# Two-layer hybrid encoder: sums of block products moved to GpSimd, half of the keys copied by transfers

## The reference

```python
h = rmsnorm(x, norm_g)
proj = jnp.einsum('bsd,de->bse', h, w_in)
aq, ak, av, ag, bq, bk, bv, bg = jnp.split(proj, SPLITS, axis=-1)
ya = chunk_relbias_attention(aq, ak, av, rel_bias) * silu(ag)   # 16 heads of 64, own chunk of 64 + previous 8
yb = swa_sink_gqa(rope(bq), rope(bk), bv, sinks) * silu(bg)     # 16 query heads, 2 key heads, window 128
x = x + concat(ya, yb) @ w_out
```

## Time and profile before

| what | value |
| --- | --- |
| median of 3 runs | 1610.96 us (1610.89 to 1611.48) |
| the profiled execution | 1612.55 us, its span 1610.2 us |
| mean granted clock of TensorE | 0.993 |
| busy: TensorE, VectorE, ScalarE, GpSimd | 99%, 79%, 59%, 30% of the span |
| HBM traffic | 109 GB/s over the span |

### The profile page before, as it was taken

The page is one execution under the profiler, slowest core; times in us unless marked ns, Lnnn a source line. Parts: engine busy times, 40 slices in busy tenths (PEclk is TensorE's granted clock), DMA queues, the critical chain, the costliest instruction groups (busy, mean ns, idle before and its releaser), DMA issues.

```text
span 1610.2 us, 29380 instructions
## 1 busy us (share of the span) xinstructions
PE 1589.0 (99%) x9541; PEld 1418.0 (88%) x9541; DVE 1276.6 (79%) x2631; ACT 954.7 (59%) x1977; POOL 477.5 (30%) x666
## 2 busy tenths in 40 slices
PE   9899999999999999999999999999999999999997
PEld 7799999999888888899988999999988888888997
DVE  7987788887677777888878788788876787888875
ACT  7766666667556666433466666766665566663333
POOL 0754454453222100010046445445422212000000
PEclk9999999999999999999999999999999999999998
DMA  6233323323523322344432332323343233223343
GB/s 223 79 97 104 109 85 109 104 90 114 167 92 95 113 88 92 105 152 157 164 104 73 107 107 91 110 90 104 109 157 112 92 107 103 79 99 112 131 144 118
DMA packets 77511, 180.69 MB, mean 112 GB/s; under 512 B 9408, under 2 KB 13792, under 8 KB 70640
## 3 DMA queue, kind: packets, MB, share of 16 engines
q1 hardware_dynamic: 76960, 178.99, 33.3%
q10 hardware_dynamic: 432, 0.55, 0.1%
q0 software_dynamic: 32, 0.08, 0.0%
HBM read 163.25 MB, written 11.62 MB: 109 GB/s over the span
## 4 chain that ended last, share of the span: by engine, by line
PE 91%; DVE 6%; DMA 1%; issue 1%; ACT 1%; SPq 0%; DVEq 0%; ACTq 0%
PE ps_proj L730 10%; PE ps_proj L732 10%; PE ps_proj L731 10%; PE ps_proj L892 4%; PE ps_proj L893 4%; PE ps_proj L894 4%; PE ps_proj L905 3%; PE ps_proj L906 2%; PE ps_proj L907 2%; PE ps_o L800 2%; PE ps_t L787 2%; PE ps_s L892 2%; PE ps_s L894 2%; PE ps_s L893 2%; PE ps_t L894 2%; PE ps_t L893 2%
## 5 line engine op out<-in xcount | busy, mean ns | idle before, releaser
L1110 ACT ACTIVATE w_hi<-w_raw 128x512 fp32r<-128x512 f32 (+1 forms) x528 | 385.7, 743 | 198.5 <-DVE w_raw L1986 62.5
L1581 DVE TENSOR_TENSOR w_lo<-w_raw,w_hi 128x512 fp32r<-128x512 f32 (+1 forms) x528 | 459.4, 878 | 34.0 <-ACT w_hi L1110 29.9
L730 PE MATMUL ps_proj<-act_hi,w_hi 128*128 128x512 f32 x704 | 276.9, 393 | 0.0
L731 PE MATMUL ps_proj<-act_lo,w_hi 128*128 128x512 f32 x704 | 274.8, 390 | 0.0
L732 PE MATMUL ps_proj<-act_hi,w_lo 128*128 128x512 f32 x704 | 274.7, 390 | 0.0
L2315 POOL TENSOR_TENSOR w_raw<-w_raw 128x128 f32<-128x128 f32 x140 | 92.0, 657 | 300.1 <-DMA w_raw<-w 299.9
L732 PEld LDWEIGHTS ps_proj<-act_hi,w_lo 128*128 128x128 f32 x704 | 132.1, 188 | 28.4
L1110 ACT ACTIVATE arena<-ps_t 128x512 fp32r<-128x512 f32 (+4 forms) x168 | 75.3, 453 | 135.3 <-PE ps_t L787 82.9
L730 PEld LDWEIGHTS ps_proj<-act_hi,w_hi 128*128 128x128 f32 x704 | 132.5, 188 | 24.8
L731 PEld LDWEIGHTS ps_proj<-act_lo,w_hi 128*128 128x128 f32 x704 | 132.4, 188 | 24.3
L1175 ACT ACTIVATE probs<-probs,nmax 128x128 f32<-128x128 f32 (+3 forms) x128 | 72.1, 563 | 97.3 <-DVE nmax L1653 95.4
(11 more groups left out here) (398 smaller groups left out, 4688.4 us busy)
## 6 DMA issues: line engine op xcount, KB each, us to landing
w_raw<-w SPq DMA_DIRECT2D x322, 256.0 KB, 3.0
w_raw<-w SPq DMA_DIRECT2D x51, 1024.0 KB, 4.9
temp<-temp SPq DMA_DIRECT2D x72, 64.0 KB, 4.0
strips_tables<-ext SPq DMA_DIRECT2D x16, 256.0 KB, 3.9
temp<-xT SPq DMA_DIRECT2D x16, 256.0 KB, 4.4
xs<-xy SPq DMA_DIRECT2D x16, 256.0 KB, 4.3
temp<-xs SPq DMA_DIRECT2D x16, 256.0 KB, 4.1
strips_tables<-ext SPq DMA_DIRECT2D x16, 224.0 KB, 4.4
```

Of the source, the lines that this page charges most:

```text
L730: pe.matmul(dst, wh, act_hi[:, k, :], start=start, stop=False)
L731: pe.matmul(dst, wh, act_lo[:, k, :], start=False, stop=False)
L1110: return nc.scalar.activation(dst, src, ACT.Copy, scale=scale)
L1581: return nc.vector.tensor_tensor(dst, src, hi, ALU.subtract)
```

## The change

- ScalarE now copies the whole bank of P1 and P6 to `in_w1`, VectorE the whole bank of P5 and P7, halves exchanged, to `in_w2` (`move_products`), and GpSimd makes the four additions there (`sum_products`), behind piece 10's weight sums for the first pair and behind piece 2's of the next unit for the second. TensorE waits for the two copies in place of the sums.
- `hi_k` and `lo_k` fill one half of the partitions each; two transfers of 256 KB per unit, issued by SP (`copy_k`), fill the other. SP issues them behind the load of piece 20. TensorE waits for their landing.
- At the start of a layer the row sums' lows 2, 3 and 4 move behind the take of the last tile and into pieces 0 and 1 of unit 1, and the reciprocal of the root moves ahead of that piece's weight subtraction.

```diff
-H_SUMS_AT = (10, 11, 12, 14, 15)
+H_SUMS_AT = (10, 11, 13, 14)
+H_SUMS_AFTER = {1: 1, 3: 2, 4: 4}
+KEYS_BEHIND = 20
...
+            def copy_k(v):
+
+                sp.wait_ge(k_done, v + 1)
+                carry_wait(sp)
+                for h in range(2):
+                    own, other = slice(64 * h, 64 * h + 64), slice(64 - 64 * h, P - 64 * h)
+                    sp.dma_start(k_st[other, :, h, :].bitcast(F32), k_st[own, :, h, :].bitcast(F32)).then_inc(k_copied, 16)
...
                 load_strips(L, 0)
+                copy_k(L * V_LAYER)
                 for j in range(4, Y_BEHIND):
                     load_in(T, L, 1, j)
...
                         if j == STRIPS_BEHIND:
                             load_strips(L, u)
+                        if j == KEYS_BEHIND:
+                            copy_k(L * V_LAYER + u)
...
                 load_strips(L, PAIRS - 1)
+                copy_k(L * V_LAYER + (PAIRS - 1))
...
                 for s in range(4):
+                    if s == 3:
+                        copy_k(L * V_LAYER + PAIRS)
                     prefetch(T + A_SLOTS, s)
...
                 if e == 0:
                     pe.wait_ge(q_done, g + 1)
-                    pe.wait_ge(k_done, v + 1)
+                    pe.wait_ge(k_copied, (v + 1) * 32)
...
                     if i == 0:
-                        pe.wait_ge(in_summed, q * 4 + 4)
+                        pe.wait_ge(in_copied, q + 1)
+                        pe.wait_ge(in_moved, q + 1)
...
                 for h in range(2):
-                    for half in range(2):
+                    for half in (h,):
                         last = copy(k_hi2[64 * half:64 * half + 64, h, :], t_k[64 * h:64 * h + 64, :])
...
                 else:
                     act.wait_ge(h_summed, (L * (IN_SUM_K - 1) + m) * 4)
-                    act.wait_ge(h_sum_lo, (L * IN_SUM_K + m) * 2)
+                if m in H_SUMS_AFTER:
+                    act.wait_ge(h_sum_lo, (L * IN_SUM_K + H_SUMS_AFTER[m]) * 2)
...
-                copy(in_w1[:, 0:SEQ // 2], in_banks(p // 8)[1][0][:, 0:SEQ // 2]).then_inc(in_copied, 1)
+                copy(in_w1, in_banks(p // 8)[1][0][:, :]).then_inc(in_copied, 1)
...
+                    if p == 1 and first:
+                        hi_h_sums(L, IN_SUM_K - 1)
...
-                    for half in range(2):
+                    for half in (h,):
                         last = low(k_lo2[64 * half:64 * half + 64, h, :], t_k[own, :], k_hi2[own, h, :].bitcast(F32))
...
-            def sum_of_products_in(L, u, p):
...
+            def move_products(L, u, p):
+
+                in_passed(dve, L, u, p // 8 * 8 + 5)
+                bank_of = in_banks(p // 8)[1][1][:, :].rearrange("p (h c) -> p h c", h=2)
+                dst = in_w2.rearrange("p (h c) -> p h c", h=2)
+                nc.vector.tensor_copy(dst[:, ::-1, :], bank_of).then_inc(in_moved, 1)
...
-                dve.wait_ge(in_summed, q * 4 + 8)
+                dve.wait_ge(in_summed, q * 4 + 4)
...
-                    if p == 0 and first:
-                        lo_h_sums(L, IN_SUM_K - 1)
+                    if p < 2 and first:
+                        lo_h_sums(L, p + 3)
...
+                        if p == 2 * PTS + 2:
+                            invert_root(L)
                         if p == 3 * PTS:
                             take_rstd(L)
                         duties(T, L, p, ("a_first", pair_a(L, 0), L * V_LAYER))
...
-                        if p == 2 * PTS + 2:
-                            invert_root(L)
-                        if p in H_SUMS_AT[:-1]:
+                        if p in H_SUMS_AT[:2]:
                             lo_h_sums(L, H_SUMS_AT.index(p))
                 dve.wait_ge(k_done, L * V_LAYER + 1)
                 take(T, 3, t_v, ps=ps_t[1])
                 dve.wait_ge(proj_free, T + 4)
                 dve.sem_inc(rows_added, 2)
+                lo_h_sums(L, 2)
...
+            def sum_products(L, u, half):
+
+                q = pair_in(L, u, half * 8)
+                (w1l, w1r), (w2l, w2r) = left_right(in_w1), left_right(in_w2)
+                pool.wait_ge(in_copied, q + 2)
+                carry_wait(pool)
+                pool.wait_ge(in_moved, q + 2)
+                carry_wait(pool)
+                nc.gpsimd.tensor_tensor(w1r, w1l, w1r, ALU.add).then_inc(in_summed, 1)
+                pool.wait_ge(in_summed, q * 4 + 1)
+                nc.gpsimd.tensor_tensor(w2l, w2l, w1r, ALU.add).then_inc(in_summed, 1)
+                pool.wait_ge(in_summed, q * 4 + 2)
+                nc.gpsimd.tensor_tensor(w1r, w2r, w1r, ALU.add).then_inc(in_summed, 1)
+                pool.wait_ge(in_summed, q * 4 + 3)
+                nc.gpsimd.tensor_tensor(w2r, w2r, w2l, ALU.add).then_inc(in_summed, 1)
+
+            def sums_of_unit(L, u, first=False):
+                for j in range(16):
+                    if IN_CHUNKS[j % 8][0] == "s":
+                        sum_w_in(L, u, j)
+                    if j == 2 and not first:
+                        sum_products(L, u - 1, 1)
+                    if j == 10:
+                        sum_products(L, u, 0)
```

More of the change, by code:

```diff
@@ L233, in trunk @@
         in_copied = sem("in_copied")
+        in_moved = sem("in_moved")
         in_summed = sem("in_summed")
@@ L269, in trunk @@
         k_done = sem("k_done")
+        k_copied = sem("k_copied")
         swapped = sem("swapped")
@@ L809, in scores_b @@
                 if n == 0:
-                    pe.wait_ge(k_done, L * V_LAYER + V_LAYER)
+                    pe.wait_ge(k_copied, (L * V_LAYER + V_LAYER) * 32)
                 pe.wait_ge(biased, step_b(L, n))
@@ L1069, in _ @@
                     unit_sums(T + u * 4, L, u, att_a(L, u - 1))
-                pe.wait_ge(in_summed, (L + 1) * (IN_PAIRS * 4) + 4)
+                pe.wait_ge(in_copied, (L + 1) * IN_PAIRS + 1)
+                pe.wait_ge(in_moved, (L + 1) * IN_PAIRS + 1)
                 unit(T + A_SLOTS, att_a(L, PAIRS - 1))
@@ L1338, in copy_p1, with unit_sums @@
                 act.wait_ge(rows_added, q * 2 + (2 * L + 2))
-                copy(in_w1[:, 0:SEQ // 2], in_banks(p // 8)[1][0][:, 0:SEQ // 2]).then_inc(in_copied, 1)
-            def unit_sums(T, L, u, att, g):
+                copy(in_w1, in_banks(p // 8)[1][0][:, :]).then_inc(in_copied, 1)
+            def unit_sums(T, L, u, att, g, first=False, last=False):
                 for p in range(16):
                     def other():
-                        if isinstance(u, int) and p + HI_AHEAD >= 16:
+                        if last and p + HI_AHEAD >= 16:
                             hi_next(tile0(L) + A_SLOTS, L, p + HI_AHEAD - 16)
@@ L1423, in squares_first @@
                     nc.scalar.activation(sq_first(j), xy[:, j, :], ACT.Square).then_inc(sq_done, 1)
+            act.sem_inc(in_copied, 1)
             act.dma_start(gain_sb[:, :], gains).then_inc(gains_in, 16)
@@ L1488, in _ @@
                         duties(T, L, p, ("a_first", pair_a(L, 0)))
-                with act.Fori(1, PAIRS - 1) as u:
+                unit_sums(T + 4, L, 1, att_a(L, 0), pair_a(L, 1), first=True)
+                with act.Fori(2, PAIRS - 1) as u:
                     unit_sums(T + u * 4, L, u, att_a(L, u - 1), pair_a(L, u))
-                unit_sums(T + (PAIRS - 1) * 4, L, PAIRS - 1, att_a(L, PAIRS - 2), pair_a(L, PAIRS - 1))
+                unit_sums(T + (PAIRS - 1) * 4, L, PAIRS - 1, att_a(L, PAIRS - 2), pair_a(L, PAIRS - 1), last=True)
                 unit(T + A_SLOTS, L, att_a(L, PAIRS - 1), ("b", None))
@@ L1808, in lo_next @@
                 low(w_lo[:, 0, chunk(c)], w_raw[:, 0, chunk(c)], w_hi[:, 0, chunk(c)].bitcast(F32)).then_inc(w_lo_done, 1)
-            def sum_of_products_in(L, u, p):
-                q = pair_in(L, u, p)
-                done = q * 4 + 4
-                (p1, p6), (p5, p7) = (left_right(b) for b in in_banks(p // 8)[1])
-                (w1l, w1r), (w2l, w2r) = left_right(in_w1), left_right(in_w2)
-                dve.wait_ge(in_copied, q + 1)
-                nc.vector.tensor_tensor(w2r, p6, w1l, ALU.add).then_inc(in_summed, 1)
-                dve.wait_ge(in_summed, done + 1)
-                nc.vector.tensor_tensor(w2l, p7, w2r, ALU.add).then_inc(in_summed, 1)
-                nc.vector.tensor_tensor(w1r, p5, w2r, ALU.add).then_inc(in_summed, 1)
-                dve.wait_ge(in_summed, done + 3)
-                nc.vector.tensor_tensor(w2r, p5, w2l, ALU.add).then_inc(in_summed, 1)
+            def move_products(L, u, p):
[3 more added lines that the diff above has]
+                nc.vector.tensor_copy(dst[:, ::-1, :], bank_of).then_inc(in_moved, 1)
             QUERIES_KEYS = ((t_q, 1.0), (t_k, 1.0))
@@ L1867, in unit_sums @@
                     if p % 8 == SUM_AT:
-                        sum_of_products_in(L, u, p)
+                        move_products(L, u, p)
                     if p == LO_Q_AT:
@@ L2094, in take_rstd @@
                 dve.wait_ge(rstd_done, L + 1)
-            dve.sem_inc(in_summed, 4)
```

(9 more changed lines are left out.)

## The result

| | kernel before | changed kernel |
| --- | --- | --- |
| median | 1611.22 us (1610.89 to 1611.56, 4 runs) | 1677.69 us (1676.13 to 1678.98, 4 runs) |
| ratio of the times | 1 | 1.0413 (95% interval 1.0400 to 1.0426) |
| span of the profiled run | 1610.2 us | 1675.0 us |
| mean granted clock | 0.993 | 0.985 |

Slower by 66.5 us, where 7.6 were forecast: the sign was right, the size wrong by a factor of nearly nine, and the time lies 48 us above the range.

A forecast was written before the change was run, and what follows sets the result against it. TensorE, busy 99% of the span, was taken as the bound. Terms 0 + 0 + 0.8 + 3.6 + 3.2 = +7.6 us on the median 1610.96 gave 1618.6 us; range 1609 to 1630.

The forecast's parts named there:

- What bounds the kernel: TensorE, busy 49.00 us of a 49.00 us steady unit; relieving VectorE and ScalarE there gains nothing.
- Part 1: Sums of block products moved to GpSimd in each half unit: put at 0, from 0 to +0.4 us a half.
- 1.0 us late: Mid-unit, GpSimd finishes the product sums at 186.2, while VectorE wants them at 185.24.
- the queue catches up within the half: GpSimd's three weight sums behind the product sums recover the delay, since GpSimd idled 300 us for its loads.
- Rival C: GpSimd late, VectorE and ScalarE waiting, attention chain missing its turn: +11 us, about +19 with parts 3 to 5; chance 0.13.
- Part 2: Half the key copies go: VectorE saves 1.7 us a unit, worth nothing by itself in a steady unit.
- Part 3: Layer starts: -0.2 us in each layer, +1.2 us clock loss in layer 0; +0.8 us, from -2.4 to +4.
- Part 4: Following units' keys: landing 3.5 us against 3.2 available, 0.3 us late 12 times; +3.6 us, from 0 to +14.
- Part 5: Last A unit's key copies wait behind two big transfers: 1.6 us late in each layer, +3.2 us.
- The weight tile queued behind their wait [...]: 0: On SP's queue behind the wait for mixer B's keys: issued in the order of VectorE's later splits, cost 0.

The follow-up runs named there:

- e7: Changed kernel with sums of products back on VectorE and key copies issued ahead of piece 20's load: 1625.77 us, ratio 1.0089 to the kernel before.
- e9: e7 with the last A unit's key copies issued ahead of its strips: 1617.54 us, ratio 1.0043 to the kernel before.
- e10: e9 with each layer's first keys copied by ScalarE and VectorE instead of by transfers: 1617.76 us, ratio 1.0047 to the kernel before.
- e1: Changed kernel with sums of products back on VectorE, keys still copied by transfers: 1643.42 us, ratio 1.0206 to the kernel before.
- e5: Changed kernel with SP issuing the key copies ahead of piece 20's load instead of behind it: 1642.46 us, ratio 1.0198 to the kernel before.
- e4: Changed kernel with GpSimd's first four additions behind piece 11's weight sum instead of piece 10's: 1651.23 us, ratio 1.0246 to the kernel before.
- e6: Changed kernel with key copies ahead of piece 20's load and GpSimd's first four additions behind piece 11's weight sum: 1632.89 us, ratio 1.0134 to the kernel before.
- e8: Changed kernel with keys copied by ScalarE and VectorE, GpSimd's first four additions behind piece 11's weight sum: 1637.08 us, ratio 1.0162 to the kernel before.

## Why the prediction was right or wrong

**What bounds the kernel**: right. TensorE's 49.06 us a unit is a floor that relief of VectorE and ScalarE did not lower in any run.

**Part 1, sums of products, put at 0**: this is the step that failed most, 27 us alone and 33 in the full change. The duration was right: 1094 + 1127 + 864 + 751 ns (the four groups below), 3.84 us, and 0.08 from each to the next, against 3.9. The end, "1.0 us late", was of the right size too: in the unit shown the last plain product was done at 193.67 and the sums at 194.92. (My addition had a slip: 181.98 + 0.65 is 182.6, not 182.3, which makes it 1.3 us late.) What failed is "the queue catches up within the half".

```profile
L2351 POOL TENSOR_TENSOR temp<-temp 128x256 f32<-128x256 f32 x28 | 31.6, 1127 | 2.2
L2349 POOL TENSOR_TENSOR temp<-temp 128x256 f32<-128x256 f32 x28 | 30.6, 1094 | 57.0 <-DVE temp L1840 32.7 <-ACT temp L1130 24.3
L2353 POOL TENSOR_TENSOR temp<-temp 128x256 f32<-128x256 f32 x28 | 24.2, 864 | 2.2
L2355 POOL TENSOR_TENSOR temp<-temp 128x256 f32<-128x256 f32 x28 | 21.0, 751 | 2.2
```

I read GpSimd's 300 us of idle time as room. But it idled for loads that come at the pace of VectorE's splits, four pieces ahead, so a sum cannot be made sooner to make up for one made late; and the change adds waits for the two copies at the head of its queue, which I did not count: 57.0 us in the second row, of which the 32.7 in fourteen first pairs stand ahead of weight sums that ScalarE wants, and the 24.3 behind a layer's last weight sum hold up none. A block of 6.4 us (188.5 to 194.9) fell between two weight sums that ScalarE wants one piece of 3.1 us apart.

**Rival C** named this mechanism whole: VectorE at the head of its queue for the product sums, ScalarE for weight sums, the turn late. It had 0.13, its point of decision was wrong (it was to need additions of over 4.5 us, and came true at 3.9). Its price of 0.4 us a half, 11 us, is what the turn alone lost (11.0); all of it came to 27 alone.

**Part 2**: right; the two subtractions took 1.82 us, the two saved are worth nothing.

**Part 3, start of a layer, +0.8**: the chain held to a tenth (keys split at 56.8 against 56.7, the second copy issued about 57.6 against 57.7). The landing was 3.9 us, not 3.0, and the scores came at 61.50 against 60.7. The idle time ahead of them was 5.52 us, not about 3, as TensorE had come free at 56.0. The extra loss of clock, put at 1.2 us, was there too. In e7, where the transfers stand alone, TensorE ran at the lower level for 5.2 us from its first scores on, which loses 2.6 us against 1.7 before:

```profile
61.20:66.40 5.20, 5.18 (x13) 4.12 (x14) 3.27 (x9) 3.13 (x5) 4.89 (x9) 0.50 0.26 93
```

Still layer 0's first unit took 51.6 us in e7 and e9 against 52.01 before, in part because the wait for the first weights (0.95 us) was gone (53.9 in the full change, with GpSimd's delays in it). In sum nothing that the medians of e9 and e10 can tell.

**Part 4, +3.6**: the chain was right again. In e1 the second copy was issued 3.25 us before TensorE asked (211.50 and 214.75), against a forecast of 3.2. The landing took 4.7 us, where I took 3.5: late by 1.43 us in that unit and by 0.75 to 1.84 in the twelve, not 0.3. The mis-sized term is the landing, and the upper bound, from the strips (4.4 us, late by 1.2), was the nearer row: same place behind a load, same form. Twelve units came to 19 us (21 by the traces), beyond the +14 of that bound too. The estimate by the Trainium skill (DMA: Bandwidth & Descriptors, Anatomy of one DMA), 2.6 us for 256 KB, was further off, and the prediction stretched it: the section states its fit for transfers that GpSimd issues, and these are SP's. The rule on that page of the Trainium skill (Rules for kernel authors) that two transfers to disjoint partition halves serialize would fit the long landing, but no run here sent one copy in place of two.

**Part 5, +3.2 for the last A units**: 7 us by the edit that took them back (e9). The keys came at 410.39 in e7 against the 408.4 forecast, landing 7.5 us after the second issue, and the clock took 1.7 us on top, which I had not priced behind a wait of that size. "The weight tile queued behind their wait [...]: 0" for mixer B failed: it cost 6 us through the swap, which stands behind that tile on SP's queue and which I did not follow.

**Sum.** Transfers +33 against 7.6; GpSimd +27 against 0; together 6 more. The sign was right although the largest term had been put at nothing. Much of the clock's 13 us belongs to late keys in a chain that GpSimd had already made late: e5, with the keys in time, has 0.990 to 0.993. The range left out C's upper part, and no rival let two delays meet.

## What to carry to other kernels

Idle time of an engine that waits for loads is not room in its queue: ask what its work can be ahead of, and put an added block, with the wait at its head, where the next instruction behind it is wanted last (27 us in e4, 10 in e6, but hardly 2 in e8). A copy by transfer that replaces one by an engine costs nothing if it lands in time and over a microsecond a unit if it doesn't; count its place in the issuing queue, take its landing from the row with other transfers ahead of it, and then follow everything that the new wait holds up behind it. Where one line decides the place, it is cheap to move: two such lines took 45 of the 66 us back (e6).

## What the runs showed of the hardware

- Key copies of 256 KB within SBUF landed in a median of 4.0 us over all 36 (page of the changed kernel). From the issue of the second to TensorE's start it was 4.6 to 4.8 us in the steady units of layer 0, behind a load, and 3.9 with nothing ahead; in the last A unit of e7, behind strips and 1 MB loads, 7.7 (402.71 to 410.39).
- TensorE's clock fell to 1.2 GHz for about 3.5 us after waits of 1.67 and 3.08 us, and did not after 1.72, 1.86 and 2.72 us. In the changed kernel five of the seven units behind the first were hit in layer 0, and three of seven in layer 1 (granted 0.66 over 5 us, against 1.00 in the others). The length of a wait alone doesn't decide it; what does was not settled.
- GpSimd's addition of 128x256 took 0.73 to 0.75 us three times in the block shown and 1.47 once (191.83), 0.96 in the mean of all, while the last of its four instructions on 128x128 (L2339, before L2320) rose from 0.65 to 0.82 us in the mean. What slows single ones was not tried.
